# GpSimd makes the depthwise convolution's fourth channel tile, VectorE the other three

## Chip, cores and metric

The kernel runs on one core of a Trainium2 chip. The metric is the device time of one execution in microseconds; the times given are of several executions, and the profile is of one of them. The engines of the core are TensorE (PE, with its weight loads as PEld), VectorE (DVE), ScalarE (ACT), GpSimd (POOL) and SyncE (SP), which here only starts transfers.

## What is computed

A trunk of two layers over 256 tokens of width 1024, float32. Each layer mixes tokens in three branches (attention over a sliding window, a convolution module, a state space model), and then channels in a gated feed-forward part. The part that the change touches, cut from the reference:

```python
def conformer_conv(a, b, w_dw, b_dw, ln_g, ln_b, w_pw):
    u = a * jax.nn.sigmoid(b)
    y = lax.conv_general_dilated(
        u, w_dw[:, None, :].astype(u.dtype), window_strides=(1,),
        padding=[(CONV_KERNEL - 1, 0)],
        dimension_numbers=('NWC', 'WIO', 'NWC'),
        feature_group_count=CONV_WIDTH) + b_dw
    y = jax.nn.silu(layernorm(y, ln_g, ln_b))
    return y @ w_pw
...
        proj = h @ w_in[l]
        q, k, v, ca, cb, su, gates = jnp.split(
            proj, [OFF_K, OFF_V, OFF_CA, OFF_CB, OFF_SU, OFF_G], axis=-1)
...
        y_conv = conformer_conv(ca, cb, conv_dw_w[l], conv_dw_b[l], conv_ln_g[l], conv_ln_b[l], conv_pw_w[l])
...
        mixed = gate_a * y_attn + gate_c * y_conv + gate_s * y_ssm
        x = x + g1 * (mixed @ w_out[l])
```

The convolution is causal, has 31 taps, 512 channels, and one weight per channel and tap. Its layer norm runs over the 512 channels.

## The kernel before

**Weights and blocks.** All large products are made from two halves of each operand, a rounded one and the rest, with three matmuls per tile (L568 to L570, in `hi_lo`). The weights of a layer are cut into 55 blocks of 128x2048 numbers each, in the order of `NAMES`. For each block SP loads `raw`, ScalarE rounds it to `whi` (L1058), VectorE subtracts to `wlo` (L1391, in `lo`), and TensorE then runs the block (`main_block`). There are four `raw`, three `whi` and two `wlo` buffers. `wlo` of block i + 2 is made when TensorE is done with block i, and stands in VectorE's stream behind the side work of block i and ahead of the block's own results (`post`).

**Side work.** Each engine's stream is one list in program order, and the small steps are placed in it by hand, in half-blocks: `side(l, t)` runs what is due at half-block t on that engine. On TensorE the even ones stand ahead of a block, the odd ones in its middle. In the stretch in question there are, on all engines, the end of the state space model, the attention's four rounds of scores and softmax, and the convolution; between the blocks also products of the modulation's weights (L604).

**The convolution.** Blocks `cb` and `ca` make the two operands; VectorE multiplies them into `uc` (L1705 in `post`, two channel tiles per block), which has 30 zero columns ahead of its 256 tokens. Channels are on partitions, so that the 512 channels are four tiles of 128x256. `conv(l, pair, seg)` makes four taps (`seg` 0 to 7, three taps in the last) of two tiles (`pair` 0 or 1). The first tap is a TENSOR_SCALAR with weight and bias (L1672), each other one a SCALAR_TENSOR_TENSOR, `yc = uc shifted * weight + yc` (L1676). The two tiles take turns, and an instruction waits for the one two before it (the same tile's last tap), so that one is always under way. The 16 segments are spread by `CONV_AT` over half-blocks 20 to 42, pair 0 first.

**After it.** At half-block 46, ahead of a block, TensorE sums over the channels with a matrix of ones (`conv_stat`, L765). It waits for `conv_ready`, set by the last tap of the last tile. The mean goes to ScalarE and VectorE (L1194, L1684), the squares are summed in the same way at half-block 48, and the normalised result enters the products of block `cp`.

**GpSimd** clears some buffers (L1017 to L1019), and for each layer clears `prod` (L1025) and doubles the columns of a loaded matrix in `uc` (L1028, a COPY). The code has a way to let it make `wlo` (L1038), which no block uses: `lo_engine` returns VectorE for all.

`crow` holds the conditioning vector c for a transpose at the start and isn't used afterwards.

Of the kernel before, what the change touches and what calls it, by code (L numbers as in the profile page):

```python
# [23 lines left out]
ALU = mybir.AluOpType  # L24
# [229 lines left out]
def trunk(nc, A, out):  # L254
    with ExitStack() as ctx:
# [3 lines left out]
        def sem(name):  # L259
            return ctx.enter_context(nc.semaphore(name))  # L260
# [54 lines left out]
        crow = sb("crow", [DK, P])  # L315
# [68 lines left out]
        sigb_ready, uc_ready, conv_ready, csum_ready, mean_ready, cent_ready, csq_ready, cvar_ready, cstd_ready, cnorm_ready, csilu_ready, c_hi, c_lo = (  # L384
            sem(n) for n in "sigb_ready uc_ready conv_ready csum_ready mean_ready cent_ready csq_ready cvar_ready cstd_ready cnorm_ready csilu_ready c_hi c_lo".split())
# [178 lines left out]
        def _(pe):  # L564
# [193 lines left out]
            def conv_stat(l, n):  # L758

                if n == 0:  # L760
                    pe.wait_ge(at_copied, 4 * (l + 1))
                pe.wait_ge(conv_ready if n == 0 else csq_ready, l + 1)
                src = yc[:, :, :] if n == 0 else uc[:, :, 0:T]
                for c in range(CT):
                    last = mm(b_t[:, n * T:(n + 1) * T], ones[:, :], src[:, c, :], start=(c == 0), stop=(c == CT - 1), skip_group_check=True)  # L765
                last.then_inc(csum_ready if n == 0 else cvar_ready, 1)
# [249 lines left out]
        def _(pool):  # L1016
            nc.gpsimd.memset(ones[:, :], 1.0).then_inc(ones_ready, 1)  # L1017
            nc.gpsimd.memset(ca[:, :, :, :, :], 0.0).then_inc(ca_zero, 1)
            nc.gpsimd.memset(kf[:, :, :, :], 0.0).then_inc(kf_zero, 1)  # L1019
            for l in range(DEPTH):  # L1020

                pool.wait_ge(vec_tr, l + 1)
                if l:
                    pool.wait_ge(tap_tr, l + 1)
                nc.gpsimd.memset(prod[:, :, :], 0.0).then_inc(ct_zero, 1)  # L1025
                pool.wait_ge(s_cc[l], 32)
                once = csrc.rearrange("p a c (g n) -> p (a c) g n", g=2)
                nc.gpsimd.tensor_copy(once[:, :, 1, :], once[:, :, 0, :]).then_inc(c_twice, 1)  # L1028
            for l in range(DEPTH):
# [331 lines left out]
        def _(dve):  # L1361
# [304 lines left out]
            def conv(l, pair, seg):  # L1666

                for k in range(4 * seg, min(4 * seg + 4, TAPS)):
                    for c in (2 * pair, 2 * pair + 1):
# [3 lines left out]
                        else:  # L1673

                            dve.wait_ge(s_dve, step.n - 1)
                            last = V.scalar_tensor_tensor(out=yc[:, c, :], in0=uc[:, c, k:k + T], scalar=w, in1=yc[:, c, :], op0=ALU.mult, op1=ALU.add)  # L1676
                        if (k, c) == (TAPS - 1, CT - 1):
                            last.then_inc(conv_ready, 1)
                        else:
                            step(last)  # L1680
# [272 lines left out]
```

## Time and profile before

| | |
|---|---|
| median of 3 runs | 989.3 us (989.25 to 991.41) |
| profiled execution, its own time | 992.07 us |
| span of its profile | 990.3 us |
| TensorE busy | 933.4 us (94%) |
| VectorE busy | 669.5 us (68%) |
| ScalarE busy | 462.4 us (47%) |
| GpSimd busy | 9.3 us (1%) |
| mean granted TensorE clock | 0.982 |

The span goes from the first to the last instruction of the profiled execution. A busy share is an average over the whole span, and stretches of it differ. In rows on instructions, an arrow stands between what is written and what is read, L and a number is the line of the kernel, and a time in brackets is how long the engine sat idle before it and what it waited for. A row with a count merges so many instructions that follow each other; its time is from the start of the first to the end of the last. Instructions of one engine can overlap in such rows by some 0.08 us.

### The profile page before, as it was taken

The numbers are of one execution on the slowest core, as the hardware profiler recorded it, in microseconds if no ns is written. First come the engines' busy times: TensorE is split into PE (matmuls) and PEld (weight loads), VectorE is DVE, ScalarE is ACT, GpSimd is POOL, SyncE is SP. The second block draws the span as 40 slices with busy tenths as digits, with TensorE's granted clock in tenths as the row PEclk, the third lists the DMA queues.
The fourth block names the chain that finished last, engine by engine and source line by source line (L and its number), as shares of the span: only waits on it lengthen the run. The fifth ranks groups of instructions, "written<-read, shape, count | busy, mean of one in ns | idle before, by whom it ended". The sixth has DMA issues, their size and how long they took to land.

```text
span 990.3 us, 16231 instructions
## 1 busy us (share of the span) xinstructions
PE 933.4 (94%) x6917; PEld 789.2 (80%) x6917; DVE 669.5 (68%) x913; ACT 462.4 (47%) x540; POOL 9.3 (1%) x11
## 2 busy tenths in 40 slices
PE   5898999989999999999999999998999999999995
PEld 1797886666777989989998997666677799999994
DVE  4882978999577674574457666999966754454545
ACT  4684135722746556545355323573264544343432
POOL 2000000000000000000000000000000000000000
PEclk9988999999999999999999999999999999999998
DMA  8972634648796566666658345465769555555521
GB/s 356 236 251 90 212 129 165 214 132 258 263 289 247 179 213 213 213 234 214 212 176 204 93 159 181 147 213 174 243 236 344 193 171 184 200 172 195 187 86 42
DMA packets 128630, 196.13 MB, mean 198 GB/s; under 512 B 30793, under 2 KB 90705, under 8 KB 122415
## 3 DMA queue, kind: packets, MB, share of 16 engines
q1 hardware_dynamic: 128247, 195.03, 59.1%
q8 instruction: 54, 0.88, 0.4%
q14 instruction: 17, 0.14, 0.1%
q10 hardware_dynamic: 312, 0.08, 0.0%
HBM read 194.02 MB, written 1.06 MB: 197 GB/s over the span
## 4 chain that ended last, share of the span: by engine, by line
PE 55%; DVE 28%; ACT 6%; issue 4%; DMA 4%; SPq 2%; ACTq 0%; DVEq 0%
PE bank L568 15%; PE bank L569 15%; PE bank L570 15%; DVE wlo L1391 9%; DVE yc L1676 9%; DMA raw<-in_w_mod 3%; ACT whi L1058 2%; PE bank L604 2%; PE bank L663 2%; PE bank L687 1%; PE bank L827 1%; PE bank L675 1%; ACT h L1073 1%; PE bank L787 1%; SPq L451 1%
## 5 line engine op out<-in xcount | busy, mean ns | idle before, releaser
L1391 DVE TENSOR_TENSOR wlo<-raw,whi 128x2048 fp32r<-128x2048 f32 (+1 forms) x135 | 302.8, 2243 | 230.6 <-PE bank L570 186.1
L1058 ACT ACTIVATE whi<-raw 128x2048 fp32r<-128x2048 f32 x132 | 252.2, 1912 | 108.1 <-PE bank L570 46.6
L568 PE MATMUL bank<-hhi,whi 128*128 128x256 f32 x928 | 267.4, 288 | 1.1 <-DVE wlo L1391 0.8
L569 PE MATMUL bank<-hlo,whi 128*128 128x256 f32 x928 | 264.2, 285 | 0.0
L570 PE MATMUL bank<-hhi,wlo 128*128 128x256 f32 x928 | 264.1, 285 | 0.0
L568 PEld LDWEIGHTS bank<-hhi,whi 128*128 128x128 f32 x928 | 179.7, 194 | 8.2 <-issue 4.2
L569 PEld LDWEIGHTS bank<-hlo,whi 128*128 128x128 f32 x928 | 179.7, 194 | 0.6
L570 PEld LDWEIGHTS bank<-hhi,wlo 128*128 128x128 f32 x928 | 179.6, 194 | 0.0
L568 PE MATMUL bank<-whi,bhi 128*128 128x512 f32 x304 | 121.4, 399 | 2.8 <-DVE wlo L1391 2.8
L569 PE MATMUL bank<-wlo,bhi 128*128 128x512 f32 x304 | 118.8, 391 | 0.0
L570 PE MATMUL bank<-whi,blo 128*128 128x512 f32 x304 | 118.5, 390 | 0.0
L568 PE MATMUL bank<-whi,hhi 128*128 128x512 f32 x256 | 106.5, 416 | 7.4 <-DVE wlo L1391 7.4
L570 PE MATMUL bank<-whi,hlo 128*128 128x512 f32 x256 | 101.4, 396 | 0.0
L569 PE MATMUL bank<-wlo,hhi 128*128 128x512 f32 x256 | 101.4, 396 | 0.0
L1676 DVE SCALAR_TENSOR_TENSOR yc<-uc,tapv,yc 128x256 f32<-128x256 f32 x240 | 97.3, 480 | 0.1
L568 PEld LDWEIGHTS bank<-whi,bhi 128*128 128x128 f32 x304 | 57.1, 188 | 24.7 <-issue 9.0
L1270 ACT ACTIVATE bhi<-gate 128x512 fp32r<-128x512 f32 x22 | 13.9, 632 | 126.6 <-DVE gate L1750 126.6
L568 PEld LDWEIGHTS bank<-whi,hhi 128*128 128x128 f32 x256 | 49.2, 192 | 29.1 <-DVE wlo L1391 10.0
L570 PEld LDWEIGHTS bank<-whi,blo 128*128 128x128 f32 x304 | 57.1, 188 | 12.4
L569 PEld LDWEIGHTS bank<-wlo,bhi 128*128 128x128 f32 x304 | 57.2, 188 | 10.5
L604 PE MATMUL bank<-raw,cact 128*32 128x512 f32 x384 | 53.1, 630 | 11.0 <-DMA raw<-in_w_mod 7.2
L570 PEld LDWEIGHTS bank<-whi,hlo 128*128 128x128 f32 x256 | 49.0, 192 | 11.1
(258 smaller groups left out, 888.7 us busy)
## 6 DMA issues: line engine op xcount, KB each, us to landing
raw<-in_w_mod SPq DMA_DIRECT2D x48, 1024.0 KB, 5.4
raw<-in_w_ffn_in SPq DMA_DIRECT2D x44, 1024.0 KB, 5.1
raw<-in_w_in SPq DMA_DIRECT2D x38, 1024.0 KB, 7.1
raw<-in_w_ffn_out SPq DMA_DIRECT2D x22, 1024.0 KB, 5.0
raw<-in_w_out SPq DMA_DIRECT2D x8, 1024.0 KB, 8.2
raw<-in_w_in SPq DMA_DIRECT2D x16, 256.0 KB, 4.5
raw<-in_ssm_glu_b SPq DMA_DIRECT2D x4, 1024.0 KB, 8.0
raw<-in_ssm_glu_a SPq DMA_DIRECT2D x4, 1024.0 KB, 6.2
```

Source lines behind the costliest of these rows:

```text
L451: eng.dma_start(bn[:, c], A[name][l].rearrange("g n i -> (g n) i").rearrange("(s p) i -> p s i", p=P)).then_inc(s_b[l], 16)
L568: mm(o, w_hi, a_hi, start=start, stop=False, skip_group_check=True)
L569: mm(o, w_hi, a_lo, start=False, stop=False, skip_group_check=True)
L570: return mm(o, w_lo, a_hi, start=False, stop=stop, skip_group_check=True)
L604: last = mm(b_mod[32 * q:32 * q + 32, :], cact32[:, k, :], weights[:, q * 512:(q + 1) * 512], start=(k == 0), stop=(k == DK - 1), skip_gro ...
L663: last = mm(o, bl[r, a, STEPS - 1 - j, k, :], u_ssm[r, k, j * NC:(j + 1) * NC], start=(k == 0 and a == 0 and j == 0), stop=(j == STEPS - 1 ...
L675: mm(o[:, t * NC:T], kf[:, k, t, :], u_ssm[:, k, 0:(STEPS - t) * NC], start=(k % 2 == 0 and t == 0), stop=False, skip_group_check=True)
L687: last = mm(b_out[k // 2][r:r + 32, c0 + 1:c0 + NC], ca[:, a, j, 4 * k + 2 * half + q, :], s[:, a, q, k, 0:NC - 1], start=False, stop=(a = ...
L1058: fn(whi[mi % N_HI][:, :], raw[SLOT[item]][:, :], ACT.Copy).then_inc(s_hi, 1)
L1270: fn(bhi[:, a:a + 2, :], gate[:, a:a + 2, :], ACT.Copy).then_inc(act_hi, 1)
L1391: part = V.tensor_tensor(wlo[mi % N_LO][:, n], raw[SLOT[("main", *divmod(mi, NB))]][:, n], whi[mi % N_HI][:, n].bitcast(F32), ALU.subtract)
L1676: last = V.scalar_tensor_tensor(out=yc[:, c, :], in0=uc[:, c, k:k + T], scalar=w, in1=yc[:, c, :], op0=ALU.mult, op1=ALU.add)
```

## The change

GpSimd gets a function `conv_last(l)`, called once per layer after its clearing work. It waits until the taps are in place and `uc` is complete, and then makes channel tile 3: for the first tap one TENSOR_SCALAR, for each of the other 30 a product into a new buffer `tap` and a sum into `yc`, each waiting for the one before by semaphore. On VectorE pair 0 stays as it was, and pair 1 is tile 2 alone, each tap waiting for the one directly before. `conv_ready` is set by the last tap of tile 2. TensorE waits for it and for GpSimd's 31 taps before it sums over channels. `crow` becomes a part of `tap`.

```diff
--- before.py
+++ after.py
@@ -312,7 +312,8 @@
         ldt = sb("ldt", [ST, 2])
         ldtr = prod[0:ST, 0, P:2 * P]
         taps = [t[0:TAPS, a:a + 2, :].rearrange("p a b -> p (a b)") for t, a in ((yc, 2), (prod, 1))]
-        crow = sb("crow", [DK, P])
+        tap = sb("tap", [P, T])
+        crow = tap[0:DK, 0:P]
         vec = [sb(f"vec{l}", [P, VROWS]) for l in range(DEPTH)]
         ldv = [sb(f"ldv{l}", [P, ST]) for l in range(DEPTH)]
         tapv = [sb(f"tapv{l}", [P, CT, TAPS]) for l in range(DEPTH)]
@@ -381,8 +382,8 @@
             sem(n) for n in "qk_ready rot_ready rope_ready vt_ready v_ready".split())
         sc_ready, mx_ready, ex_ready, pr_ready, pt_ready, pt_copied, pv_ready, at_copied, at_hi, at_lo = (
             sem(n) for n in "sc_ready mx_ready ex_ready pr_ready pt_ready pt_copied pv_ready at_copied at_hi at_lo".split())
-        sigb_ready, uc_ready, conv_ready, csum_ready, mean_ready, cent_ready, csq_ready, cvar_ready, cstd_ready, cnorm_ready, csilu_ready, c_hi, c_lo = (
-            sem(n) for n in "sigb_ready uc_ready conv_ready csum_ready mean_ready cent_ready csq_ready cvar_ready cstd_ready cnorm_ready csilu_ready c_hi c_lo".split())
+        conv_pool, tap_pool, sigb_ready, uc_ready, conv_ready, csum_ready, mean_ready, cent_ready, csq_ready, cvar_ready, cstd_ready, cnorm_ready, csilu_ready, c_hi, c_lo = (
+            sem(n) for n in "conv_pool tap_pool sigb_ready uc_ready conv_ready csum_ready mean_ready cent_ready csq_ready cvar_ready cstd_ready cnorm_ready csilu_ready c_hi c_lo".split())
         gate_ready, ao_read, cp_read, glsig_ready, gl_read, gl_mixed = (
             sem(n) for n in "gate_ready ao_read cp_read glsig_ready gl_read gl_mixed".split())
         x_mid, x_next, silu_ready, act_ready, act_hi, act_lo, ffn_sum = (
@@ -760,6 +761,8 @@
                 if n == 0:
                     pe.wait_ge(at_copied, 4 * (l + 1))
                 pe.wait_ge(conv_ready if n == 0 else csq_ready, l + 1)
+                if n == 0:
+                    pe.wait_ge(conv_pool, TAPS * (l + 1))
                 src = yc[:, :, :] if n == 0 else uc[:, :, 0:T]
                 for c in range(CT):
                     last = mm(b_t[:, n * T:(n + 1) * T], ones[:, :], src[:, c, :], start=(c == 0), stop=(c == CT - 1), skip_group_check=True)
@@ -1017,6 +1020,22 @@
             nc.gpsimd.memset(ones[:, :], 1.0).then_inc(ones_ready, 1)
             nc.gpsimd.memset(ca[:, :, :, :, :], 0.0).then_inc(ca_zero, 1)
             nc.gpsimd.memset(kf[:, :, :, :], 0.0).then_inc(kf_zero, 1)
+            def conv_last(l):
+
+                c = CT - 1
+                pool.wait_ge(tap_cp, l + 1)
+                pool.wait_ge(uc_ready, 2 * l + 2)
+                for k in range(TAPS):
+                    w = tapv[l][:, c, k:k + 1]
+                    if k == 0:
+                        last = nc.gpsimd.tensor_scalar(yc[:, c, :], uc[:, c, 0:T], w, vec[l][:, R_DWB + c:R_DWB + c + 1], ALU.mult, ALU.add)
+                    else:
+                        pool.wait_ge(conv_pool, TAPS * l + k)
+                        nc.gpsimd.tensor_scalar(tap[:, :], uc[:, c, k:k + T], w, None, ALU.mult).then_inc(tap_pool, 1)
+                        pool.wait_ge(tap_pool, (TAPS - 1) * l + k)
+                        last = nc.gpsimd.tensor_tensor(yc[:, c, :], yc[:, c, :], tap[:, :], ALU.add)
+                    last.then_inc(conv_pool, 1)
+
             for l in range(DEPTH):
 
                 pool.wait_ge(vec_tr, l + 1)
@@ -1026,6 +1045,7 @@
                 pool.wait_ge(s_cc[l], 32)
                 once = csrc.rearrange("p a c (g n) -> p (a c) g n", g=2)
                 nc.gpsimd.tensor_copy(once[:, :, 1, :], once[:, :, 0, :]).then_inc(c_twice, 1)
+                conv_last(l)
             for l in range(DEPTH):
                 for i in range(NB):
                     if lo_engine(i) != "pool":
@@ -1666,15 +1686,15 @@
             def conv(l, pair, seg):
 
                 for k in range(4 * seg, min(4 * seg + 4, TAPS)):
-                    for c in (2 * pair, 2 * pair + 1):
+                    for c in ((0, 1), (2,))[pair]:
                         w = tapv[l][:, c, k:k + 1]
                         if k == 0:
                             last = V.tensor_scalar(yc[:, c, :], uc[:, c, 0:T], w, vec[l][:, R_DWB + c:R_DWB + c + 1], ALU.mult, ALU.add)
                         else:
 
-                            dve.wait_ge(s_dve, step.n - 1)
+                            dve.wait_ge(s_dve, step.n - (1 - pair))
                             last = V.scalar_tensor_tensor(out=yc[:, c, :], in0=uc[:, c, k:k + T], scalar=w, in1=yc[:, c, :], op0=ALU.mult, op1=ALU.add)
-                        if (k, c) == (TAPS - 1, CT - 1):
+                        if (k, c) == (TAPS - 1, CT - 2):
                             last.then_inc(conv_ready, 1)
                         else:
                             step(last)
```

## Rows read from the trace of the kernel before

**Rows 1.** The page: engines' busy time, share and instructions; then the chain by engine:

```profile
PE 933.4 (94%) x6917; PEld 789.2 (80%) x6917; DVE 669.5 (68%) x913; ACT 462.4 (47%) x540; POOL 9.3 (1%) x11
...
PE 55%; DVE 28%; ACT 6%; issue 4%; DMA 4%; SPq 2%; ACTq 0%; DVEq 0%
```

**Rows 2.** The chain that ended last, 158 to 250 us, by line:

```profile
by line: DVE yc L1676 42.9%; DVE wlo L1391 28.9%; issue 4.9%; DVE blx L1723 3.1%; DVE tmp L1721 2.8%; DVE blx L1718 2.3%; DVE blo L1696 2.2%; ACT bhi L1212 2.2%; ACT whi L1058 2.1%; DVE tmp L1716 2.0%; DVE h L1618 1.5%; ACT h L1173 1.4%; DV
```

**Rows 3.** By stretch: length, busy us (count) of PE PEld DVE ACT POOL, clock, DMA:

```profile
133.40:142.40 9.00, 9.00 (x64) 7.07 (x64) 6.24 (x13) 4.87 (x12) 0.00 (x0) 1.00 0.66 236
...
158.50:180.00 21.50, 20.50 (x120) 14.24 (x113) 21.31 (x43) 11.76 (x21) 0.00 (x0) 1.00 0.41 147
...
197.00:247.70 50.70, 45.03 (x203) 32.52 (x202) 50.26 (x85) 14.78 (x12) 0.00 (x0) 0.97 0.64 199
```

**Rows 4.** TensorE in time: start us, us, line, operation; idle before it in brackets:

```profile
167.28 0.50 PE L568 MATMUL bank<-whi,bhi 128*128 128x512 f32 x1
...
207.79 0.79 PE L568 MATMUL bank<-whi,hhi 128*128 128x512 f32 x1 [3.70 <-DVE wlo L1391]
208.38 0.63 PE L569 MATMUL bank<-wlo,hhi 128*128 128x512 f32 x1
...
211.41 0.40 PE L568 MATMUL bank<-whi,hhi 128*128 128x512 f32 x1
...
229.89 0.50 PE L568 MATMUL bank<-whi,bhi 128*128 128x512 f32 x1 [1.51 <-DVE wlo L1391]
...
681.96 0.79 PE L568 MATMUL bank<-whi,hhi 128*128 128x512 f32 x1 [3.70 <-DVE wlo L1391]
...
704.05 0.50 PE L568 MATMUL bank<-whi,bhi 128*128 128x512 f32 x1 [0.97 <-DVE wlo L1391]
```

**Rows 5.** VectorE in time, layer 0, 152 to 170 us:

```profile
152.55 1.65 DVE L1662 SCALAR_TENSOR_TENSOR u_ssm<-u_ssm,vec,bank 128x256 f32<-128x256 f32 x4
...
158.55 2.06 DVE L1696 TENSOR_TENSOR blo<-u_ssm,bhi 128x1024 fp32r<-128x1024 f32 x1 [3.14 <-ACT bhi L1212]
...
163.71 2.27 DVE L1391 TENSOR_TENSOR wlo<-raw,whi 128x2048 fp32r<-128x2048 f32 x1
165.91 3.24 DVE L1676 SCALAR_TENSOR_TENSOR yc<-uc,tapv,yc 128x256 f32<-128x256 f32 x8
169.08 0.67 DVE L1609 TENSOR_REDUCE mx<-bank 128x4 f32<-128x512 f32 x1
```

**Rows 6.** VectorE in time, 132 to 135 us:

```profile
132.67 0.68 DVE L1705 TENSOR_TENSOR uc<-bank,tmp 128x512 f32<-128x512 f32 x1
133.39 0.42 DVE L1590 TENSOR_TENSOR gate<-bank,sinr 128x256 f32<-128x256 f32 x1
133.73 0.41 DVE L1591 TENSOR_TENSOR kT<-kT,cosr 128x256 f32<-128x256 f32 x1
134.18 0.42 DVE L1592 TENSOR_TENSOR kT<-kT,gate 128x256 f32<-128x256 f32 x1
```

**Rows 7.** TensorE in time: the first sums over channels (L765), layer 0:

```profile
243.22 1.99 PE L765 MATMUL bank<-yc,ones 128*128 128x256 f32 x8
```

**Rows 8.** GpSimd's two COPYs; VectorE beside them; L1573 ns min/median/max, all its instructions:

```profile
35.95 0.61 POOL L1028 COPY uc<-uc 128x512 f32<-128x512 f32 x1 [24.68 <-DMA uc<-in_ssm_c_im]
...
35.94 0.90 DVE L1573 SCALAR_TENSOR_TENSOR hlo<-h,modv,hhi 128x256 fp32r<-128x256 f32 x1
...
L1573 DVE SCALAR_TENSOR_TENSOR hlo<-h,modv,hhi x32: 471/479/901, 35.9 to 795.4; 128x256 fp32r<-128x256 f32 x32
...
324.12 1.22 POOL L1028 COPY uc<-uc 128x512 f32<-128x512 f32 x1
...
322.57 2.29 DVE L1391 TENSOR_TENSOR wlo<-raw,whi 128x2048 fp32r<-128x2048 f32 x1 [0.87 <-PE bank L837]
```

**Rows 9.** VectorE's groups with two SBUF inputs, 142.4 to 180 us: count | busy, mean ns:

```profile
L1676 DVE SCALAR_TENSOR_TENSOR yc<-uc,tapv,yc 128x256 f32<-128x256 f32 x46 | 18.5, 476 | 0.0
L1391 DVE TENSOR_TENSOR wlo<-raw,whi 128x2048 fp32r<-128x2048 f32 x4 | 9.1, 2282 | 0.0
```

## Prediction

> **What bounds the kernel now.** I read the page first for the whole span: TensorE is busy 94% of it, VectorE 68%, and GpSimd 1% with 11 instructions [rows 1]. That alone would make VectorE work free. The chain that ended last says otherwise: 28% of it lies on VectorE [rows 1]. So I asked for the chain in the stretch of layer 0 in which the convolution runs (158 to 250 us): the conv's multiply-adds (L1676) hold 42.9% of it and the weight splits `wlo` (L1391) 28.9% [rows 2]. The table by stretch then shows how tight that is. From 158.5 to 180 us VectorE is busy 21.31 of 21.50 us and TensorE 20.50; from 197 to 247.7 us VectorE 50.26 of 50.70 and TensorE only 45.03 [rows 3]. In the rest of the span TensorE is the limit, here both are: VectorE has nothing to spare, and TensorE loses little to it.
>
> Where TensorE loses it stands in its timeline: in layer 0 it waits 3.70 us at 207.79 and 1.51 us at 229.89 for `wlo`, in layer 1 3.70 us at 681.96 and 0.97 us at 704.05. Behind the long waits seven matmuls take 0.63 us where others take 0.39, one every 0.43 instead of 0.23 us: 7 x 0.20 = 1.4 us at the lower of TensorE's two clock levels [rows 4]. That is 6.6 us in layer 0 and 6.1 us in layer 1: all that relief of VectorE can bring there. How close the other blocks are is the distance from the end of `wlo` to the block's first matmul, as 163.71 + 2.27 = 165.98 against 167.28 (1.3 us) [rows 4, 5].
>
> **What the change takes off VectorE.** 31 operations per layer on the fourth tile. Eight L1676 start at 165.91 and the next instruction starts at 169.08 [rows 5]: 3.17 / 8 = 0.396 us each, 31 x 0.396 = 12.3 us. But all of it comes off the second pair; the first pair (142.4 to 197.2 us) keeps its two tiles. And the third tile is now a single chain in which each tap waits for the one before. At the same size an instruction that doesn't wait starts 0.34 us after its forerunner (133.39 to 133.73), one that does 0.45 us (133.73 to 134.18) [rows 6]. So 30 x 0.11 = 3.3 us go back, and 9.0 us per layer remain.
>
> How much of that reaches TensorE: by the wait at 207.79 two of the eight segments of the pair are done, 8 taps, 8 x 0.396 - 8 x 0.11 = 2.3 us off the wait of 3.7. What is left, 1.4 us, should be too short for the clock to fall (the waits of 1.51 and 0.97 us had no slow matmuls behind them [rows 4]), so the 1.4 us go as well, and the later wait of 1.5 or 1.0 us goes whole. 2.3 + 1.4 + 1.25 = 5.0 us per layer. The rest of the 9.0 us becomes idle time of VectorE, since TensorE's own work then ends last.
>
> **What it adds on GpSimd.** 61 instructions per layer: one scaled and biased start, then 30 products and 30 sums, each waiting for the one before. GpSimd may begin when `uc` is whole: the second L1705 runs 132.67 to 133.35 us, and the stretch of layer 1 is built alike [rows 6]. It must be done when TensorE comes to the sums over channels (L765), 243.22 us [rows 7]. The trace has no GpSimd arithmetic, only a COPY of 128x512: 0.61 us [rows 8]. For a product (half the elements, one input) I take 0.4 us, for a sum (512 elements read) 0.61, and 0.2 us for the two semaphores: 1.2 us per tap, 37 us for all, in 110 us. Even at three times this the deadline is near but kept. So GpSimd's own time costs nothing; the cover is the distance to 243 us.
>
> **What it adds by sharing.** This is the term that decides. At 35.95 us the COPY starts, 0.61 us long, and the VectorE instruction beside it, an L1573 (128x256, two SBUF tensors in, one out, as L1676 is), takes 0.90 us; of the 32 such instructions the median is 0.479 us, and 0.901 is the longest [rows 8]. The COPY held it for 0.42 us. The reverse is there too: the other COPY starts at 324.12 while `wlo` runs (322.57 to 324.86) and takes 1.22 us, its own 0.61 and 0.61 of waiting [rows 8]. So when both engines read SBUF with such instructions, one waits for the other. By the Trainium skill (SBUF — State Buffer, section SBUF: two separate sides) a GpSimd operation and a VectorE operation with two SBUF inputs share one port pair, an exclusive lock that whoever starts first keeps for the whole instruction. Both rows agree in kind; as to size the row shows 0.42 of the COPY's 0.61 us. By the rule's "whole" the price per tap would be the upper bound below.
>
> Price per tap, when VectorE wants to run: product plus sum. Below, by what the COPY held for 512 elements (0.42): half for the product, all for the sum, 0.63 us. Above, whole durations, 0.4 + 0.61 = 1.01 us. I take the middle, 0.82, since the sum has two reads per element where the COPY has one, and nothing says that they are done in the COPY's time. The skill (GPSIMD Engine Reference, section 3.1) gives 4497 ns for a sum of 2048 elements; an estimate from it is 0.56 us for 256, with which the tap would be at 0.77 us.
>
> How many taps meet VectorE: from 133.35 to 142.4 VectorE is busy 6.24 of 9.00 us [rows 3], 2.3 of it one `wlo` that GpSimd must wait out; in the 6 us left fit 5 taps. Then VectorE runs, from 142.4 to 180 us, 46 + 4 + 3 + 1 = 54 instructions with two SBUF inputs (46 and 4 of them [rows 9], the others one to three each); but from 152.55 to 154.3 us it reads PSUM, it idles 3.14 us before 158.55 [rows 5], and with the reductions and small operations some 7 us are free of the conflict: 6 taps. 20 taps are left, 40 instructions, one in each gap between VectorE's. They are through at about the old 175 us, long before the second pair. 20 x 0.82 = 16.4 us of delay on an engine that is busy 99% of that stretch.
>
> What absorbs it: the distance found above, 1.3 us; with VectorE late anyway I count 1 us, once. The 3.14 us before 158.55 absorb nothing, being ScalarE's time behind VectorE's own results. Behind the waiting VectorE instruction stands the next `wlo`, and behind that TensorE. TensorE's slower clock after these waits is hidden, since `wlo` comes last in every block there. So 15.4 us are lost per layer before 197 us, and 5.0 come back after it: 10.4 net.
>
> **Other edits.** `crow` inside `tap`: used for one load at the start, 100 us before `tap` is written; nothing. SP's queue gets and loses nothing, no DMA is moved. TensorE's added wait for GpSimd's last sum stands at 243 us and is met about 45 us early; queued behind it would be every later block. GpSimd's next work is for layer 1's preparation, around its second COPY at 324.12 us [rows 8], and far off. VectorE's `conv_ready` comes with the third tile's last tap, its work ending earlier. All at nothing.
>
> **Sum.** 2 x (16.4 - 1.0 - 5.0) = +20.8 us. On the span of 990.3 that is 1011.1, on the profiled execution's own 992.07 it is 1012.9. The median of the runs shown, 989.3, is 2.8 us below that execution, so I forecast 989.3 + 20.8 = 1010 us. Bounds of this case: 15 taps at 0.63 with a full 6 us back, 2 x (9.5 - 1 - 6) = +5, 994 us; 26 taps at 1.01 with 4 us back, 2 x (26.3 - 1 - 4) = +43, 1032 us.
>
> **Rivals.**
> (a) Faster: VectorE is hardly held. If its instructions, queued closely, keep GpSimd waiting as the `wlo` at 322.57 did and let it in only where it costs little, the delay vanishes and the relief stays: 2 x 5.0 us off, 979 us. The place is the stretch 142 to 180 us; it decides below (1.0 + 5.0) / 20 = 0.30 us per tap. Against it: at 35.94 a VectorE instruction was queued just as closely behind a `wlo`, and it was the one that waited [rows 8].
> (b) GpSimd is starved and ends late. Then it gets only VectorE's free stretches, 5 taps before 142.4, 6 until 158.5 and about 5 in the short PSUM operations up to 243 us. 15 taps x 1.2 = 18 us are left while TensorE stands at L765: 2 x (18 - 5) = +26, 1015 us. The same row at 35.94 speaks against it.
> (c) GpSimd's arithmetic is much dearer than its COPY, say twice 0.82 per tap: 2 x (20 x 1.64 - 1 - 5) = +54, 1043 us. Nothing in the trace excludes it.
> (d) It cancels: the holding costs just the relief, 0.3 us per tap, or GpSimd's taps fall mostly in free time; 989 us.
>
> **How the numbers follow.** Forecast 0.66; (a) 0.15; (b) 0.06; (c) 0.07; (d) 0.06. A measurement of this kernel can tell about 0.3% (3 us) from no change. Faster by more is (a) and a little of (d): 0.16. Within it: most of (d), 0.05. Slower: 0.79. The range goes from (a), 979, to the upper bound with a little of (c), 1035; what is left out is most of (c) and the far side of (a).
>
> **What would show it.** Right: in the changed kernel's trace L1676 in the first pair has two classes of duration, 0.48 us and 0.7 to 1.1 us, `wlo` too is at times longer than 2.29; GpSimd's last sum is at about 190 to 200 us; TensorE has waits for `wlo` between 150 and 195 us, where it has almost none now, summing to about 15 us, and fewer after 200; the start of L765 moves from 243 to about 253 us. Wrong: L1676 all at 0.48 us (then (a)); GpSimd's last sum after 240 us and TensorE waiting for it at L765 (then (b)); GpSimd products or sums over 1 us without a VectorE instruction beside them (then (c)). If VectorE is held but L765 doesn't move, the step that takes VectorE to be the last in each block before 197 us is wrong.

## The result

The changed kernel takes 1009.42 us (median of 4 runs, 1006.37 to 1011.07) against 989.27 for the one before: ratio 1.0189, with a 95% interval of 1.0171 to 1.0207. It is 19 us slower by this ratio and 20.2 us by the two medians; the forecast was 1010 us, 20.8 slower. Run again beside later experiments it gave 1.0190 (1.0171 to 1.0209).

The page of the changed kernel, its engines' busy time, answers to [rows 1]; the costliest groups of VectorE's convolution and of GpSimd follow (L1696 is the former L1676, L1034 the product, L1036 the sum).

```profile
span 1009.3 us, 16295 instructions
PE 943.7 (94%) x6917; PEld 796.2 (79%) x6917; DVE 681.3 (68%) x851; ACT 462.3 (46%) x540; POOL 132.7 (13%) x133
...
L1696 DVE SCALAR_TENSOR_TENSOR yc<-uc,tapv,yc 128x256 f32<-128x256 f32 x180 | 99.7, 601 | 1.9
...
L1034 POOL TENSOR_SCALAR tap<-uc,tapv 128x256 f32<-128x256 f32 x60 | 67.0, 1117 | 5.9
```

VectorE runs 62 instructions fewer and is busy 11.8 us longer. The 180 multiply-adds that are left keep VectorE busy for longer (99.7 us) than the 240 of before did (97.3 us). VectorE in time, layer 0, in the stretch where GpSimd works, shows where; to be set beside [rows 5] and [rows 9].

```profile
130.35 0.68 DVE L1725 TENSOR_TENSOR uc<-bank,tmp 128x512 f32<-128x512 f32 x1
...
150.00 2.82 DVE L1411 TENSOR_TENSOR wlo<-raw,whi 128x2048 fp32r<-128x2048 f32 x1
...
170.01 5.35 DVE L1696 SCALAR_TENSOR_TENSOR yc<-uc,tapv,yc 128x256 f32<-128x256 f32 x8
...
180.69 9.91 DVE L1696 SCALAR_TENSOR_TENSOR yc<-uc,tapv,yc 128x256 f32<-128x256 f32 x16
...
207.59 2.28 DVE L1411 TENSOR_TENSOR wlo<-raw,whi 128x2048 fp32r<-128x2048 f32 x1
```

Eight multiply-adds that took 3.24 us [rows 5] take 5.35, and a `wlo` 2.82 in place of 2.29. The last row's instruction stood at 195.00 before:

```profile
195.00 2.29 DVE L1391 TENSOR_TENSOR wlo<-raw,whi 128x2048 fp32r<-128x2048 f32 x1
```

GpSimd in time, changed kernel: undisturbed taps at first, a product that waits out a `wlo` (2.84 us), and the last sum of layer 0.

```profile
133.77 0.93 POOL L1034 TENSOR_SCALAR tap<-uc,tapv 128x256 f32<-128x256 f32 x1
134.78 0.74 POOL L1036 TENSOR_TENSOR yc<-yc,tap 128x256 f32<-128x256 f32 x1
135.61 0.93 POOL L1034 TENSOR_SCALAR tap<-uc,tapv 128x256 f32<-128x256 f32 x1
...
150.78 2.84 POOL L1034 TENSOR_SCALAR tap<-uc,tapv 128x256 f32<-128x256 f32 x1
...
198.00 0.99 POOL L1036 TENSOR_TENSOR yc<-yc,tap 128x256 f32<-128x256 f32 x1
```

TensorE in time, changed kernel, its longer waits of layer 0 and then the sums over channels, to be set beside [rows 4] and [rows 7] (L742 are transposes of the attention's probabilities):

```profile
170.14 0.80 PE L569 MATMUL bank<-whi,bhi 128*128 128x512 f32 x1 [5.00 <-DVE wlo L1411]
...
181.44 0.63 PE L742 MATMUL bank<-ident,h 128*128 128x128 f32 x4 [1.94 <-ACT blx L1204]
...
199.03 0.63 PE L742 MATMUL bank<-ident,h 128*128 128x128 f32 x4 [2.62 <-ACT blx L1204]
...
218.02 0.50 PE L569 MATMUL bank<-whi,hhi 128*128 128x512 f32 x1 [1.36 <-DVE wlo L1411]
...
250.42 1.99 PE L768 MATMUL bank<-yc,ones 128*128 128x256 f32 x8
```

TensorE's waits in all (total us, times, longest), before from 130 to 197 us and after from 130 to 205:

```profile
PE bank L741 <- ACT blx L1184: 1.0, 1, 1.0
```

```profile
PE bank L569 <- DVE wlo L1411: 5.8, 2, 5.0
PE bank L742 <- ACT blx L1204: 4.6, 2, 2.6
```

1.0 us have become 10.4. What is left of the loss is in TensorE's own work. By stretch from the last product into `uc` to the `wlo` just shown, in layer 0 and in layer 1 (length, busy us (count) of PE PEld DVE ACT POOL, clock, DMA), first before and then after:

```profile
132.67:195.00 62.33, 61.33 (x417) 43.66 (x416) 55.03 (x113) 37.47 (x66) 0.00 (x0) 1.00 0.52 182
...
611.02:669.17 58.15, 56.32 (x277) 39.25 (x277) 51.42 (x109) 34.65 (x64) 0.00 (x0) 0.97 0.56 195
```

```profile
130.35:207.59 77.24, 66.85 (x415) 47.21 (x414) 70.83 (x114) 37.20 (x66) 62.29 (x61) 0.91 0.42 148
...
617.09:692.96 75.87, 64.53 (x276) 45.07 (x276) 67.78 (x108) 34.40 (x64) 60.94 (x61) 0.87 0.43 150
```

In layer 0 TensorE is idle for 1.0 us of the stretch before and for 10.4 after, and its matmuls, the same but for two records, keep it busy 5.5 us longer, with the granted clock at 0.91 instead of 1.00: 9.4 + 5.5 = 14.9 us. After 205 us the waits of 3.70 and 1.51 us [rows 4] have become one of 1.36 us and one of 0.20.

**Where the 19 us lie.** The three marks are the last product into `uc`, the `wlo` just shown and the first sum over channels, each as after less before. Layer 0: 130.35 - 132.67 = -2.3, 207.59 - 195.00 = +12.6, 250.42 - 243.22 = +7.2 us. So the stretch shared with GpSimd cost 14.9 us and the rest gave 5.4 back. In layer 1 the same marks stand before (the last row: ns min/median/max, then the first and the last start, which is layer 1's) and after at

```profile
611.02 0.69 DVE L1705 TENSOR_TENSOR uc<-bank,tmp 128x512 f32<-128x512 f32 x1
...
669.17 2.29 DVE L1391 TENSOR_TENSOR wlo<-raw,whi 128x2048 fp32r<-128x2048 f32 x1
...
L765 PEld LDWEIGHTS bank<-yc,ones x16: 186/190/190, 243.2 to 718.8; 128*128 128x128 f32 x16
```

```profile
617.09 0.69 DVE L1725 TENSOR_TENSOR uc<-bank,tmp 128x512 f32<-128x512 f32 x1
...
692.96 2.29 DVE L1411 TENSOR_TENSOR wlo<-raw,whi 128x2048 fp32r<-128x2048 f32 x1
...
L768 PEld LDWEIGHTS bank<-yc,ones x16: 186/190/190, 250.4 to 737.6; 128*128 128x128 f32 x16
```

(the last start is not layer 1's first one, but the same instruction in both), that is +6.1, +23.8, +18.8: 17.7 us lost, 5.0 back. That is 9.5 + 12.7 = 22.2 us. Against it stand the 2.3 us by which this execution was early before GpSimd began, and 1.1 us between the layers. Both lie within the scatter between executions. In the experiments below, whose kernels are alike up to that point, the last product into `uc` starts anywhere from 128.9 (experiment 11) to 131.5 us (experiment 8), and in the profile of before at 132.67, later than in all of them. From the sum over channels of layer 0 to that product in layer 1 it is 367.8 us before and 366.7 after, and between 366.7 and 368.6 in the other profiles.

### The profile page after: what moved, and what is told of

Same layout as the page of the kernel before. It is cut to its first block, busy times and chain, and to the rows that moved or that the text cites. A ratio compares the mean times of both kernels' runs of the same rounds, so it can differ in the third digit from the quotient of the medians.

```text
span 1009.3 us, 16295 instructions
## 1 busy us (share of the span) xinstructions
PE 943.7 (94%) x6917; PEld 796.2 (79%) x6917; DVE 681.3 (68%) x851; ACT 462.3 (46%) x540; POOL 132.7 (13%) x133
## 4 chain that ended last, share of the span: by engine, by line
PE 62%; DVE 25%; ACT 5%; issue 4%; DMA 4%; SPq 0%; ACTq 0%; DVEq 0%
PE bank L569 17%; PE bank L571 17%; PE bank L570 17%; DVE yc L1696 7%; DVE wlo L1411 7%; DMA raw<-in_w_mod 3%; PE bank L605 2%; ACT whi L1078 2%; PE bank L830 2%; PE bank L664 1%; PE bank L688 1%; PE bank L676 1%; DMA raw<-in_w_in 1%; PE bank L840 1%; ACT h L1093 1%
## 5 line engine op out<-in xcount | busy, mean ns | idle before, releaser
L569 PE MATMUL bank<-whi,bhi 128*128 128x512 f32 x304 | 124.9, 411 | 6.2 <-DVE wlo L1411 6.2
L570 PE MATMUL bank<-wlo,bhi 128*128 128x512 f32 x304 | 122.2, 402 | 0.0
L571 PE MATMUL bank<-whi,blo 128*128 128x512 f32 x304 | 121.8, 401 | 0.0
L1696 DVE SCALAR_TENSOR_TENSOR yc<-uc,tapv,yc 128x256 f32<-128x256 f32 x180 | 99.7, 601 | 1.9
L569 PEld LDWEIGHTS bank<-whi,bhi 128*128 128x128 f32 x304 | 59.6, 196 | 28.3 <-DVE wlo L1411 9.7
L571 PEld LDWEIGHTS bank<-whi,blo 128*128 128x128 f32 x304 | 59.2, 195 | 13.2
L570 PEld LDWEIGHTS bank<-wlo,bhi 128*128 128x128 f32 x304 | 59.4, 195 | 11.3
L1034 POOL TENSOR_SCALAR tap<-uc,tapv 128x256 f32<-128x256 f32 x60 | 67.0, 1117 | 5.9
```

What stands on the lines that cost most here:

```text
L569: mm(o, w_hi, a_hi, start=start, stop=False, skip_group_check=True)
L570: mm(o, w_hi, a_lo, start=False, stop=False, skip_group_check=True)
L571: return mm(o, w_lo, a_hi, start=False, stop=stop, skip_group_check=True)
L1034: nc.gpsimd.tensor_scalar(tap[:, :], uc[:, c, k:k + T], w, None, ALU.mult).then_inc(tap_pool, 1)
```

## Experiments

All ran beside the kernel before; a ratio is to that kernel on the same chip. The differences shown are to the changed kernel in experiments 1, 2, 7 and 11, to the kernel of experiment 1 in experiments 3 to 6, and to the kernel before in 8 to 10; of each only the main lines are shown.

**1. The cost without the relief** (`share_only`). GpSimd works on a spare buffer `acc`, whose content nobody uses, and VectorE makes all four tiles.

```diff
-                        last = nc.gpsimd.tensor_tensor(yc[:, c, :], yc[:, c, :], tap[:, :], ALU.add)
+                        last = nc.gpsimd.tensor_tensor(acc[:, :], acc[:, :], tap[:, :], ALU.add)
...
-                    for c in ((0, 1), (2,))[pair]:
+                    for c in (2 * pair, 2 * pair + 1):
```

> GpSimd makes its 61 instructions per layer at the same time as in the change, but into a spare buffer (its result is not used), and VectorE makes all four channel tiles as before. So this is the change's cost without its relief. Theory (each of GpSimd's instructions that reads SBUF holds up a VectorE instruction with two SBUF inputs): the change's +19.9 us plus the relief of 2 x 5.0 that is now missing, about 1019 us; VectorE is held for about 15 us per layer ahead of 200 us. Rival (the change lost its time through the third tile's single chain or TensorE's added wait): about 989 us.

1020.76 us, ratio 1.0312 (1.0283 to 1.0340), +30.9 us. VectorE has the same 913 instructions as before and is busy 31.4 us longer (669.5 before):

```profile
PE 946.5 (93%) x6917; PEld 797.0 (78%) x6917; DVE 700.9 (69%) x913; ACT 461.9 (45%) x540; POOL 132.6 (13%) x133
```

31.4 us of holding and 30.9 us of time: in this stretch VectorE's time is the kernel's time. So the change doesn't lose through the third tile's single chain, which this kernel hasn't got. TensorE's wait for GpSimd is still in it; what rules that out is the trace, in which GpSimd's last sum starts at 197.84 us here, as at 198.00 in the change, long before TensorE sums over channels.

**2. The relief without the cost** (`relief_only`). 30 of the 31 taps of tile 3 are left out, so that the kernel doesn't compute the convolution in full.

```diff
-                for k in range(TAPS):
+                for k in range(1):
...
-                    pe.wait_ge(conv_pool, TAPS * (l + 1))
+                    pe.wait_ge(conv_pool, l + 1)
```

> VectorE as in the change (three tiles, the third as a single chain); GpSimd makes only the first tap of the fourth tile, so that 30 taps of that tile are left out. Theory: the relief alone, 2 x 5.0 us off, 979 us; TensorE's waits for wlo between 197 and 247 us are gone. Rival (the single chain costs what the missing tile gives): 989 us.

978.03 us, ratio 0.9884 (0.9860 to 0.9907), -11.8 us. Added to experiment 1 this gives +19.1 us, against +20.2 for the change by the medians: the two parts add within the scatter of the runs. TensorE's waits for `wlo` over the whole span, before and here:

```profile
PE bank L568 <- DVE wlo L1391: 11.0, 7, 3.7
```

```profile
PE bank L569 <- DVE wlo L1411: 4.3, 7, 1.4
```

The longest went from 3.7 to 1.4 us, the value that the prediction worked out for it.

**3. Instructions as long that read nothing** (`clears`).

```diff
-                        nc.gpsimd.tensor_scalar(tap[:, :], uc[:, c, k:k + T], w, None, ALU.mult).then_inc(tap_pool, 1)
+                        nc.gpsimd.memset(wide[:, 0:992], 0.0).then_inc(tap_pool, 1)
...
-                        last = nc.gpsimd.tensor_tensor(acc[:, :], acc[:, :], tap[:, :], ALU.add)
+                        last = nc.gpsimd.memset(wide[:, 0:752], 0.0)
```

> As the run in which GpSimd works beside a VectorE with all four tiles, but the 30 products and 30 sums per layer are clears (MEMSET) of 992 and 752 elements, which take about as long (0.93 and 0.73 us) and read nothing. Theory (what is fought over is reading SBUF): 989 to 992 us and no VectorE instruction lengthened. Rival (any GpSimd access, or its semaphore traffic, holds VectorE up): near 1019 us.

992.74 us, ratio 1.0035 (1.0020 to 1.0049). VectorE's groups in this run:

```profile
L1414 DVE TENSOR_TENSOR wlo<-raw,whi 128x2048 fp32r<-128x2048 f32 x129 | 295.5, 2291 | 226.1 <-PE bank L573 183.6 <-ACT whi L1081 38.8 <-PE bank L842 3.4
L1699 DVE SCALAR_TENSOR_TENSOR yc<-uc,tapv,yc 128x256 f32<-128x256 f32 x240 | 97.3, 482 | 0.1
```

97.3 us as before, and `wlo` at its 2291 ns: GpSimd's writes, waits and semaphores hold no instruction with two SBUF inputs. The Trainium skill (SBUF — State Buffer, section SBUF: two separate sides) says of VectorE instructions with two SBUF inputs that they conflict only with GpSimd operations that read SBUF; this run agrees for these. But the clears do hold two other kinds, each with one SBUF tensor in: the first taps and the softmax's negated maximum, ns min/median/max, before and here:

```profile
L1672 DVE TENSOR_SCALAR yc<-uc,tapv,vec x8: 405/408/415, 142.4 to 672.3; 128x256 f32<-128x256 f32 x8
...
L1612 DVE TENSOR_SCALAR nmx<-mx x8: 161/162/165, 137.6 to 657.1; 128x4 f32<-128x4 f32 x8
```

```profile
L1695 DVE TENSOR_SCALAR yc<-uc,tapv,vec x8: 404/542/1091, 138.8 to 670.0; 128x256 f32<-128x256 f32 x8
...
L1635 DVE TENSOR_SCALAR nmx<-mx x8: 164/351/815, 133.9 to 654.2; 128x4 f32<-128x4 f32 x8
```

A first tap takes up to 1.09 us where it took 0.41, and VectorE is busy 671.9 us in all, 2.4 more than before. The time is 3.5 us above before (0.35%). That these holds are its cause is likely but not shown.

**4. The same work where VectorE has room** (`later`).

```diff
-                pool.wait_ge(uc_ready, 2 * l + 2)
-                pool.wait_ge(s_ready, 2 * l + 2)
+                if l:
+                    pool.wait_ge(conv_pool, TAPS * l)
+                pool.wait_ge(act_lo, l * NF + 6)
```

(and the operands a table and GpSimd's own buffer, both layers' work after GpSimd's other tasks, and TensorE no longer waits for it)

> VectorE makes all four tiles as before; GpSimd makes 61 instructions per layer of the same kinds and sizes, on a table and its own buffer, but begins in the feed-forward part, after its sixth block pair, where VectorE is busy about half of the time. Its result is not used. Theory (a held VectorE costs time only where it is at its limit): 989 to 993 us although VectorE instructions are held there too. Rival (each hold costs its length wherever it falls): VectorE is held 61 x 0.3 us or so per layer at half the chance, +15 to +20 us.

990.45 us, ratio 1.0007 (0.9993 to 1.0021). The page has VectorE busy 675.3 us, 5.8 more than before, and the product's group on GpSimd shows the fight:

```profile
L1036 POOL TENSOR_SCALAR tap<-sinr,tapv 128x256 f32<-128x256 f32 x60 | 78.5, 1308 | 5.9
```

1308 ns on average for 925 undisturbed, mostly waiting out `wlo`. VectorE was held and it cost nothing. The holds are also fewer than in experiment 1 (31.4 us); what the run tells is that these 5.8 us had no price, where there nearly every microsecond had one. Most of them lie in layer 0: from 421 to 508 us VectorE is busy 52.15 us, before 47.89, and TensorE all 87 us in both. In layer 1 (887 to 972 us) VectorE is busy 40.85 and 40.86 us, so that hardly anything was held there.

**5 and 6. Which instruction holds for how long** (`products`, `sums`). GpSimd's 60 instructions per layer behind the first are all products, or all sums; VectorE makes four tiles.

```diff
-                        last = nc.gpsimd.tensor_tensor(acc[:, :], acc[:, :], tap[:, :], ALU.add)
+                        last = nc.gpsimd.tensor_scalar(acc[:, :], uc[:, c, k:k + T], w, None, ALU.mult)
```

```diff
-                        nc.gpsimd.tensor_scalar(tap[:, :], uc[:, c, k:k + T], w, None, ALU.mult).then_inc(tap_pool, 1)
+                        nc.gpsimd.tensor_tensor(tap[:, :], acc[:, :], uc[:, c, k:k + T], ALU.add).then_inc(tap_pool, 1)
```

> As the run in which GpSimd works beside a VectorE that makes all four tiles, but all of GpSimd's 61 instructions per layer are products (one SBUF tensor in; 0.93 us each when nothing is in the way), its result unused. In that run VectorE's busy time was 31.4 us above before. Theory A (a hold lasts as long as GpSimd streams its elements: 0.21 us for a product, the rest of the 0.7 for a sum): about 40 of 60 products meet VectorE, 40 x 0.21 = 8.6 us per layer, in all about +15 us, 1005 us. Theory B (every instruction that reads SBUF holds alike, about 0.4 us): 40 x 0.42 = 17 us per layer, +31 us, 1021 us.

> The same with 60 sums (two SBUF tensors in; 0.73 us each) in place of products and sums, its result unused. Theory A (length of the stream; a sum reads twice as much): 40 x 0.5 = 20 us per layer, +38 us, 1028 us. Theory B (all alike): 40 x 0.42 = 17 us per layer, +31 us, 1021 us.

Products: 1006.77 us, ratio 1.0171 (1.0153 to 1.0189). Sums: 1031.48 us, 1.0423 (1.0401 to 1.0444). VectorE's multiply-adds, ns min/median/max, of which the maximum tells the longest hold; first beside products and then beside sums:

```profile
L1699 DVE SCALAR_TENSOR_TENSOR yc<-uc,tapv,yc x240: 470/493/705, 140.2 to 724.1; 128x256 f32<-128x256 f32 x120
```

```profile
L1699 DVE SCALAR_TENSOR_TENSOR yc<-uc,tapv,yc x240: 468/487/1018, 142.1 to 749.1; 128x256 f32<-128x256 f32 x120
```

Undisturbed it is 480 ns. A product holds VectorE for up to 705 - 480 = 225 ns, a sum for up to 1018 - 480 = 538 ns, together 0.76 us. This is the upper end. In the changed kernel itself, where products and sums alternate, the longest of the 180 multiply-adds takes 967 ns:

```profile
L1696 DVE SCALAR_TENSOR_TENSOR yc<-uc,tapv,yc x180: 471/485/967, 141.5 to 728.1; 128x256 f32<-128x256 f32 x180
```

There a sum holds for up to 0.49 us and a tap costs 0.225 + 0.487 = 0.71 us. Theory A's numbers came out (1005 and 1028 us) and theory B's (1021 us for both) did not: the hold isn't alike for all, and it isn't the length of the instruction, which is 0.92 us for the product and 0.73 for the sum. That it is the time in which the operands are streamed fits, since the sum reads two tensors and holds more than twice as long, but no run shows the streaming itself. One product of the changed kernel shows that the hold ends early: the multiply-add beside it starts 0.10 us after it and takes 0.695 us, so that it is over at 144.01, ahead of the product (144.18).

```profile
143.21 0.97 POOL L1034 TENSOR_SCALAR tap<-uc,tapv 128x256 f32<-128x256 f32 x1
...
L1696 DVE SCALAR_TENSOR_TENSOR yc<-uc,tapv,yc x1: 695/695/695, 143.3 to 143.3; 128x256 f32<-128x256 f32 x1
```

VectorE's busy time rose by 18.5 and 44.7 us (688.0 and 714.2 on the pages): at the longest holds 18.5 / 0.225 = 82 and 44.7 / 0.538 = 83 of the 120 instructions met VectorE, and more if many held for less.

**7. The relief put where the cost is** (`even3`).

```diff
-CONV_AT = {20 + 3 * n // 2: divmod(n, 8) for n in range(16)}
+CONV_AT = {20 + 2 * n: n for n in range(12)}
...
-                    for c in ((0, 1), (2,))[pair]:
+                    for c in range(CT - 1):
```

(and `conv` makes the taps from 31 n / 12 to 31 (n + 1) / 12 for part n)

> The change, with VectorE's three tiles spread evenly: every one of 12 blocks gets 2 or 3 taps of all three tiles (93 tap operations, three chains in turns) in place of two tiles in the first half and one in the second. Theory: VectorE is held as before (15 us per layer), but now it has 16 tap operations less in the stretch in which it is held (6.3 us) and as many more after it, where it has room; and the single chain's 3.3 us are gone. So about 6 us per layer better than the change, 997 us. Rival (what counts is the attention rounds' place between the taps, not their number): no better than 1009.

997.24 us, ratio 1.0074 (1.0052 to 1.0096). 12 us of the 20.2 between the medians are gone with GpSimd's part untouched, by moving VectorE's own taps out of the stretch that it shares. The single chain of the third tile went with it, and the two are not separated here. It is still slower than before.

**8 and 9. Without GpSimd: VectorE's time bought elsewhere** (`act_first`, `seg_earlier`). `seg_earlier` is the kernel before with one segment at half-block 22 in place of 23; `act_first` is that and ScalarE making the first taps.

```diff
+CONV_AT[22] = CONV_AT.pop(23)
```

```diff
+            def conv_first(l):
+                act.wait_ge(tap_cp, l + 1)
+                act.wait_ge(uc_ready, 2 * l + 2)
+                for c in range(CT):
+                    last = fn(yc[:, c, :], uc[:, c, 0:T], ACT.Identity, scale=tapv[l][:, c, 0:1], bias=vec[l][:, R_DWB + c:R_DWB + c + 1])
+                last.then_inc(first_ready, 1)
```

> The kernel before, without GpSimd's part, with two small moves: the first tap of all four tiles is made by ScalarE (Identity with a scale and a bias per partition) in its idle time before the first softmax round, and one segment of the convolution stands a half-block earlier on VectorE (22 in place of 23), ahead of the wait of 3.1 us for ScalarE. Theory (VectorE's time in this stretch is what counts): 4 x 0.33 = 1.3 us per layer off it, and in layer 0 3.1 us of idle time filled: 2.6 + 3.1 = 5.7 us, 984 us. Rival (TensorE's waits sit elsewhere): 989.

> The kernel before with one segment of the convolution a half-block earlier on VectorE (22 in place of 23) and nothing else. Theory: it fills the wait of 3.1 us for ScalarE that stands ahead of the state space model's split in layer 0; layer 1 has no such wait there. So 3.1 of the 6 us of the run with both moves are its, 986 us; the first taps on ScalarE have the other 2.6. Rival: all of that run's gain is from ScalarE's taps, 989 us.

Both: 983.38 us, ratio 0.9940 (0.9921 to 0.9961). The segment alone: 985.19 us, 0.9943 (0.9928 to 0.9958). Both are faster than the kernel before. The wait of 3.14 us [rows 5] in the run with the segment alone:

```profile
150.67 3.25 DVE L1677 SCALAR_TENSOR_TENSOR yc<-uc,tapv,yc 128x256 f32<-128x256 f32 x8
...
155.13 2.06 DVE L1697 TENSOR_TENSOR blo<-u_ssm,bhi 128x1024 fp32r<-128x1024 f32 x1 [0.18 <-ACT bhi L1213]
```

It is down to 0.18 us. But I had expected 3.1 us of this run, all in layer 0, and it gave 4.7 by the medians and 5.7 by the ratio. Layer 1, which has no such wait, gained too. Its stretch from the last product into `uc` to the same `wlo` as above took 58.15 us before with VectorE busy for 51.42; here it is

```profile
604.84:659.63 54.79, 52.95 (x269) 36.72 (x269) 51.31 (x109) 33.29 (x64) 0.00 (x0) 1.00 0.59 207
```

so that VectorE idles 3.5 us in place of 6.7, with the same work. Which of its waits the earlier segment filled there is left open, and scatter between executions has a part in it (56.8 us in experiment 2, with the same VectorE work in this stretch as before). That ScalarE's first taps add the 2.6 us that I expected of them isn't shown: the ratios differ by 0.03%.

**10. Only six taps on GpSimd, begun while VectorE has free time** (`easy_six`). Both moves, and taps 1 to 6 of tile 3 on GpSimd.

```diff
+                for k in range(1, EASY + 1):
+                    if k > 1:
+                        pool.wait_ge(conv_pool, EASY * l + k - 1)
+                    nc.gpsimd.tensor_scalar(tap[:, :], uc[:, c, k:k + T], tapv[l][:, c, k:k + 1], None, ALU.mult).then_inc(tap_pool, 1)
+                    pool.wait_ge(tap_pool, EASY * l + k)
+                    nc.gpsimd.tensor_tensor(yc[:, c, :], yc[:, c, :], tap[:, :], ALU.add).then_inc(conv_pool, 1)
```

> Both moves of the earlier run (first taps on ScalarE, one segment at half-block 22), and GpSimd makes taps 1 to 6 of the fourth tile, a product and a sum each, which it begins when VectorE is still partly idle; VectorE makes taps 7 to 30 of it. Theory: 6 x 1.84 us of GpSimd run from about 134 to 145 us, and two of the six taps meet the convolution's start, 2 x 0.76 us, part of it in idle time; VectorE has 6 x 0.396 us less after 197 us, less 6 x 0.11 for the single chain: 1.7 off and 0.5 to 1.5 on per layer, so 0.5 to 2.5 us below the run without GpSimd (983.4), about 982 us. Rival (GpSimd's part costs whatever its size, as it did for 30 taps): above 983.4.

984.31 us, ratio 0.9936 (0.9922 to 0.9951), beside the segment alone (0.9943): no difference that these runs can tell. It isn't the 982 us that I expected, nor can the runs tell it from the 983.4 us without GpSimd. The heavy price is gone: what six taps cost is made good by what they relieve, where thirty lose 19 us. GpSimd's first product starts at 134.19 and its last sum at 146.57 us, so that the last taps do meet the convolution, and VectorE is held there:

```profile
140.97 6.62 DVE L1704 SCALAR_TENSOR_TENSOR yc<-uc,tapv,yc 128x256 f32<-128x256 f32 x10
```

Ten multiply-adds take 6.62 us, where eight took 3.24 [rows 5].

**11 and 12. A shorter product** (`short_product`, beside the changed kernel, `after_again`).

```diff
-                        nc.gpsimd.tensor_scalar(tap[:, :], uc[:, c, k:k + T], w, None, ALU.mult).then_inc(tap_pool, 1)
+                        nc.gpsimd.tensor_scalar(tap[:, :], uc[:, c, k:k + T], w, 0.0, ALU.mult, ALU.add).then_inc(tap_pool, 1)
```

> The change, with GpSimd's product written as a multiply and an add of zero: the first tap, which has both operations, took 0.55 us where the products with the multiply alone take 0.92, at any offset. If that holds for the products, GpSimd is done 30 x 0.37 = 11 us earlier per layer. Theory (what costs is how long an instruction streams against VectorE, 0.22 us for a product, not how long it lasts): the hold per tap stays 0.76 us, one tap or two more fall in VectorE's idle time ahead of the convolution, 2 x 1 us, so 1007 us against the change's 1009. Rival (GpSimd's own duration is part of the price): 2 x 20 x 0.37 = 15 us less, 994 us.

> The changed kernel itself, on the same chip as the run with the shorter product, for the comparison of the two: 1009 us.

1006.32 us, ratio 1.0177 (1.0146 to 1.0207), and the change beside it 1008.77 us, 1.0190. The product, ns min/median/max, in the first profile of the changed kernel and here:

```profile
L1034 POOL TENSOR_SCALAR tap<-uc,tapv x60: 924/974/2845, 131.9 to 682.4; 128x256 f32<-128x256 f32 x60
```

```profile
L1034 POOL TENSOR_SCALAR tap<-uc,tapv x60: 478/530/2654, 130.5 to 667.8; 128x256 f32<-128x256 f32 x60
```

GpSimd needs 25.6 us less (busy 106.9 against 132.5 us), VectorE is busy the same 682.2 and 682.4 us, and the time is the same within the intervals. The rival, 994 us, is far outside. GpSimd's own time is not the price.

## Why the prediction was right, step by step

The forecast of 20.8 us and the 20.2 between the medians lie closer together than the terms behind them: a price that was taken too high and a number of taps that was taken too low cancelled to within 0.6 us per layer, which is luck. The mechanism, and the sign and rough size of each term, stand on the runs.

**The bound.** Right. One reading was too strong: the 99% holds from 158.5 to 180 us, but from 142.4 to 180 VectorE is busy 33.75 of 37.60 us (90%), the 3.14 us of idle time included. VectorE's longer busy time came out as time, 31.4 us of it as 30.9 us (experiment 1), where the share of 68% for the whole span suggested room.

**The relief, 5.0 us per layer.** Measured 5.4 and 5.0 us between the marks, and 5.9 alone (experiment 2, half of 11.8). The price of the single chain was right as well: from 229.01 to 233.05 us eight taps of the third tile take 4.04 us, 0.505 each, for the 0.396 + 0.11 of the prediction. The 3.7 us wait left 1.4 as worked out, and no slow matmuls stand behind it.

**The price per tap, 0.82 us.** Too high. Measured 0.71 in the changed kernel, at most 0.76 (experiments 5 and 6). I took the middle between what the COPY had held and whole durations. The lower model was the better one for the product: 0.225 us by measurement, 0.21 by half of the COPY's 0.42. The sum holds 0.49 to 0.54 where the COPY's row gave 0.42. The Trainium skill's figure for a long sum (GPSIMD Engine Reference, section 3.1) led to an estimate of 0.77 us per tap; the trace is at or a little below that. With the rule of the Trainium skill (SBUF — State Buffer, section SBUF: two separate sides) as I put it, that the pair is kept for the whole instruction, the trace does not agree: the product lasts 0.92 us and holds 0.22.

**The number of taps, 20.** Too low. VectorE is busy 681.3 us in the change and 649.7 in experiment 2, which has the same VectorE instructions: 31.6 us, 15.8 per layer, and 15.8 / 0.71 = 22 taps. This is a count in whole holds, worked out and not read. I gave GpSimd 1.2 us per tap, and undisturbed it needs 1.84 (133.77 to 135.61), as the product takes 0.93 and not 0.4, so that fewer taps fit in the free stretches than the 5 and 6 that I counted. And the small operations that I took to be free of the conflict are held too: the softmax's negated maximum, 0.16 us before, takes up to 0.73 in the changed kernel.

```profile
L1632 DVE TENSOR_SCALAR nmx<-mx x8: 163/166/731, 135.6 to 679.6; 128x4 f32<-128x4 f32 x8
```

GpSimd ended layer 0 at 199.0 us, at the late edge of what I had named (190 to 200). Price times number, 16.4 us in the prediction, is 15.8.

**What absorbs it, 1.0 us.** 16.4 - 1.0 = 15.4 us were to be lost by 197 us. Measured: 14.9 in layer 0 and 17.7 in layer 1, where the holds make 15.8 on average. The 2 us on top in layer 1 didn't come again. In the second profile of the changed kernel (`after_again`) the same stretches are

```profile
129.64:206.80 77.16, 68.03 (x415) 48.38 (x413) 70.77 (x114) 37.18 (x66) 62.22 (x61) 0.89 0.42 147
616.53:690.03 73.50, 62.46 (x274) 43.44 (x274) 68.65 (x109) 34.28 (x64) 60.95 (x61) 0.88 0.44 154
```

that is 14.8 and 15.4 us more than before. In layer 1 this stretch differs by 2 to 3 us between executions also where VectorE does the same work and is hardly held (56.8 us in experiment 2, 58.6 in experiment 3, 59.6 in experiment 4), so that the absorbed microsecond is too small to be tested there.

**The waits' place.** Half wrong. I named waits for `wlo` of about 15 us from 150 to 195 us. They are 5.8 us, and 4.6 us are waits of the attention's transposes for ScalarE; over the whole span these went from 1.0 to 13.1 us. ScalarE in time, changed kernel:

```profile
195.02 0.37 ACT L1193 ACTIVATE h<-bank,nmx 128x128 f32<-128x128 f32 x1 [8.89 <-DVE nmx L1632]
...
196.50 1.92 ACT L1078 ACTIVATE whi<-raw 128x2048 fp32r<-128x2048 f32 x1
198.30 0.59 ACT L1204 ACTIVATE blx<-bank 64x512 f32<-64x512 f32 x1
```

The held VectorE gives the softmax's maximum late (`nmx`, 8.89 us waited for here, up to 13.8 in the whole run, where the longest of before was 7.2), ScalarE makes its exponentials and then a weight split ahead of the small copy (L1204) on which TensorE's next transpose waits. The lateness reaches TensorE through the attention as much as through the weights. The sum wasn't hurt by it, since both ways carry the same delay. The dropping clock was said to be hidden, and for the sum it was: the loss in layer 0 is no larger than what VectorE was held. But it is why the waits add up to 10.4 us and not to 15: the matmuls took 5.5 us more in that stretch, at a granted clock of 0.91 (the table above), and where they are slow TensorE has less left to wait.

**The rivals.** (a) needed less than 0.30 us per tap and (d) 0.30; it is 0.71. (b) is out: GpSimd ends 51 us before TensorE needs it. (c) was half there, in a harmless form: the arithmetic is dearer on GpSimd than the COPY suggested, but that isn't what VectorE pays. Experiment 11 shows this.

## What to carry to other kernels

Work that is moved from VectorE to GpSimd is paid by VectorE as long as both stream from SBUF: ask what the GpSimd form holds per unit of work (here 0.71 us) against what VectorE needed for it (0.396 us); if it is more, the move loses where VectorE is at its limit, however idle GpSimd looks. One odd instruction in the trace of the kernel before, 0.90 us where the median of its kind is 0.48, gave the kind of the price and nearly its size. What helped a full VectorE here was to fill its waits (experiments 8 and 9) and to take its own work out of the shared stretch (experiment 7).

## What the runs showed of the hardware

- The hold ends before GpSimd's instruction does: 0.225 us of 0.92 for a 128x256 product, 0.49 to 0.54 of 0.73 for a 128x256 sum.
- GpSimd's clears of 0.93 and 0.73 us hold no VectorE instruction with two SBUF inputs, but they do hold its TENSOR_SCALARs from SBUF to SBUF: 1.09 us at most in place of 0.41 for 128x256, 0.82 in place of 0.16 for 128x4 (experiment 3).
- GpSimd, in turn, waits for a whole `wlo`: its product takes up to 2.84 us then.
- On GpSimd a TENSOR_SCALAR of 128x256 with a multiply alone takes 0.92 us, with a multiply and an add 0.55 (first tap) or 0.48 to 0.53 (experiment 11).
